# Diffusion step with a PEER expert mixer on one core: the V stage's third and fourth group are loaded ahead of the wait for all gate stores

## What is computed

```python
experts = (i1 * PEER_KEYS + i2).reshape(nch, PEER_CHUNK, PEER_HEADS * PEER_TOPK)
...
        h = jax.nn.gelu(jnp.einsum('tkd,td->tk', u[ec], xc))
        return jnp.einsum('tk,tkd->td', gc * h, v[ec])
```

## Time and profile before

| | |
|---|---|
| Median of 3 runs | 3056.86 us (3056.62 to 3060.37) |
| The profiled execution's own time | 3059.12 us |
| Its span | 3057.6 us |
| TensorE busy | 2904.8 us, 95% of the span |
| VectorE busy | 1813.5 us, 59% |
| ScalarE busy | 1203.6 us, 39% |
| V stage of layer 1 (first to last start of an L699 matmul) | 986.8 to 1518.7 us |
| V stage of layer 2 | 2498.7 to 3031.0 us |
| Mean granted clock of TensorE | 0.978 |

### The profile page before, as it was taken

One profiled execution on the slowest core, in us unless ns is written; L12 is line 12 of the kernel. 1 busy time (PEld: TensorE's weight loads), 2 busy tenths in 40 slices (PEclk: granted clock), 3 DMA queues, 4 the chain that ended last, 5 costly groups with the idle time before them and its releaser, 6 DMA issues.

```text
span 3057.6 us, 48767 instructions
## 1 busy us (share of the span) xinstructions
PE 2904.8 (95%) x16962; PEld 2660.9 (87%) x16962; DVE 1813.5 (59%) x4002; ACT 1203.6 (39%) x2024; POOL 10.0 (0%) x21
## 2 busy tenths in 40 slices
PE   6898999999999999999988989999999999999997
PEld 5877999999999788888778789999999997888886
DVE  3344387776875555555534444878777745555555
ACT  3343334344344344444323434443443433434443
POOL 0000000000000000000000000000000000000000
PEclk8998999999999999999989999999999999999999
DMA  6262353764847766666454524547558387666661
GB/s 272 104 235 86 121 177 120 221 195 132 261 153 239 277 227 219 226 229 222 151 218 145 186 84 142 162 129 239 179 153 260 116 276 269 227 219 226 230 221 64
DMA packets 256736, 581.68 MB, mean 190 GB/s; under 512 B 13025, under 2 KB 209889, under 8 KB 211617
## 3 DMA queue, kind: packets, MB, share of 16 engines
q1 hardware_dynamic: 255360, 571.81, 54.8%
q0 software_dynamic: 1184, 7.34, 0.6%
HBM read 475.82 MB, written 103.28 MB: 189 GB/s over the span
## 4 chain that ended last, share of the span: by engine, by line
PE 90%; DMA 3%; DVE 2%; issue 2%; ACT 1%; SPq 1%; ACTq 0%; DVEq 0%
PE ps L660 33%; PE ps L699 33%; PE ps L550 11%; PE ps L681 6%; PE ps L567 1%; PE ps L515 1%; PE ps L493 1%; PE ps L625 1%; PE ps L642 1%; DMA act_scratch<-act_h 1%; DMA gate_scratch<-g_all 1%; PE ps L614 1%; DMA wring<-in_w_ada_dram 1%; PE ps L595 1%; DVE u_lo L1150 0%
## 5 line engine op out<-in xcount | busy, mean ns | idle before, releaser
L660 PE MATMUL ps<-h_lo,u_hi 128*128 128x384 f32 x2048 | 697.0, 340 | 13.7 <-DVE u_lo L1150 5.8
L660 PE MATMUL ps<-h_hi,u_lo 128*128 128x384 f32 x2048 | 688.1, 336 | 0.0
L660 PE MATMUL ps<-h_hi,u_hi 128*128 128x384 f32 x2048 | 687.4, 336 | 0.0
L699 PE MATMUL ps<-v_lo,w_hi 128*128 128x512 f32 x1536 | 600.5, 391 | 15.8 <-DVE v_lo L1291 15.2
L1291 DVE TENSOR_TENSOR v_lo<-wring,v_hi 128x512 fp32r<-128x512 f32 x512 | 354.6, 693 | 435.6 <-ACT v_hi L924 435.4
L699 PE MATMUL ps<-v_hi,w_hi 128*128 128x512 f32 x1536 | 599.7, 390 | 0.0
L699 PE MATMUL ps<-v_hi,w_lo 128*128 128x512 f32 x1536 | 599.5, 390 | 0.0
L924 ACT CAST v_hi<-wring 128x512 fp32r<-128x512 f32 x512 | 316.8, 620 | 598.0 <-PE ps L699 597.9
L1150 DVE TENSOR_TENSOR u_lo<-wring,u_hi 128x1024 fp32r<-128x1024 f32 x256 | 313.2, 1223 | 208.7 <-ACT u_hi L881 205.3
L660 PEld LDWEIGHTS ps<-h_lo,u_hi 128*128 128x128 f32 x2048 | 386.5, 189 | 18.7 <-DVE u_lo L1150 10.3
L660 PEld LDWEIGHTS ps<-h_hi,u_hi 128*128 128x128 f32 x2048 | 386.5, 189 | 0.0
(11 more groups left out here) (162 smaller groups left out, 2971.8 us busy)
## 6 DMA issues: line engine op xcount, KB each, us to landing
wring<-in_u_t_dram SPq DMA_DIRECT2D x128, 1024.0 KB, 5.6
wring<-in_v_t_dram SPq DMA_DIRECT2D x128, 1024.0 KB, 4.9
wring<-in_w_ada_dram SPq DMA_DIRECT2D x48, 1024.0 KB, 6.8
act_scratch<-act_h SPq DMA_DIRECT2D x256, 192.0 KB, 5.8
gate_scratch<-g_all SPq DMA_DIRECT2D x48, 1024.0 KB, 6.4
gate<-gate_scratch SPq DMA_DIRECT2D x64, 768.0 KB, 6.3
act<-act_scratch SPq DMA_DIRECT2D x64, 768.0 KB, 7.9
wring<-in_w_in_dram SPq DMA_DIRECT2D x20, 1024.0 KB, 5.2
```

The lines of the kernel that those rows point to most:

```text
L660: last = nc.tensor.matmul(ps[:, 6 + s % 2, 0:T], u[:, s % 2, k], hx[:, k], start=(k == 0 and n == 0), stop=(k == KC - 1 and n == 2))
L699: last = nc.tensor.matmul(ps[:, bank + tb], w[:, group * G + b, cols], v[:, n % 4], start=(first and n in (0, G) and k == 0), stop=(last_u ...
```

## The change

Three edits, all in SyncE's list. Pieces 5, 6 and 7 are taken out of `TAIL_PIECES`. The definition of `group_loads` moves up, and it is called for groups 2 and 3 ahead of the wait for all stores; piece 5 is stored after group 2's loads, pieces 6 and 7 after group 3's. The loop over the other groups begins at 4. Because groups 2 and 3 are now loaded before the wait for all activation stores, the earlier wait on `act_st`, ahead of group 0's load, asks for the first 16 blocks where it asked for 8.

```diff
-TAIL_PIECES = {2: (3,), 3: (4,), 4: (5, 6, 7)}
+TAIL_PIECES = {2: (3,), 3: (4,)}
...
                     for sig in act_st:
-                        sp.wait_ge(sig.sem, sig.at(l, 16 * (2 * G // AR)))
+                        sp.wait_ge(sig.sem, sig.at(l, 16 * (4 * G // AR)))
                         sp.sem_inc(sp_passed.sem, 1)
...
+            def group_loads(g, n, ga=True):
+
+                if ga:
+                    sp.wait_ge(w32_rdy.sem, l * NB + (g - 1) * G)
+                    load_ga(g, n)
+                for half in range(2):
+                    slot = 2 * n + half
+
+                    sp.wait_ge(vlo_rdy.sem, l * NV + (g * (2 * G) + (G * (half - 3) + vlo_rdy.credit)))
+                    load_v(g, half, slot)
+
+            for n in range(2):
+                group_loads(2 + n, n)
+                for piece in ((5,), (6, 7))[n]:
+                    store_gates(TB - 1, piece)
             for sig in g_st[3:]:
                 sp.wait_ge(sig.sem, sig.at(l, 16 * TB))
                 sp.sem_inc(sp_passed.sem, 1)
...
-            with sp.Fori(1, NG // 2) as i:
+            with sp.Fori(2, NG // 2) as i:
                 for n in range(2):
                     group_loads(i * 2 + n, n)
```

More of the change, by code:

```diff
@@ L435, in _ @@
                     load_ga(1, 1)
[L436 to L441, removed]
             def group_loads(g, n, ga=True):
@@ L452, in group_loads @@
                     load_v(g, half, slot)
-            with sp.Fori(1, NG // 2) as i:
+            for n in range(2):
+                group_loads(2 + n, n)
+                for piece in ((5,), (6, 7))[n]:
+                    store_gates(TB - 1, piece)
+            for sig in g_st[3:]:
+                sp.wait_ge(sig.sem, sig.at(l, 16 * TB))
+                sp.sem_inc(sp_passed.sem, 1)
+            for sig in act_st:
+                sp.wait_ge(sig.sem, sig.at(l, 16 * (NB // AR)))
+                sp.sem_inc(sp_passed.sem, 1)
+            with sp.Fori(2, NG // 2) as i:
                 for n in range(2):
```

## The result

The changed kernel takes 3035.98 us (median of 6 runs, 3033.14 to 3040.92), the kernel before, run beside it, 3058.23 us (3055.54 to 3062.28). The ratio is 0.9929, with a 95% interval of 0.9916 to 0.9942: faster by 0.7%. Predicted were 3037.0 us and a range of 3033 to 3043. The profiled execution took 3040.92 us, the longest of the six.

The account below looks back on a forecast made before the run. TensorE, busy for 95% of the span, was taken to bound the kernel. Removing V-stage stalls of 9.7 + 10.1 = 19.8 us and adding 0 takes the profiled 3059.12 to 3039.3, or 3037.0 for the median; range 3033 to 3043.

Parts of the forecast that it names:

- What bounds, and what the stall costs: V stage: TensorE bounds; its stall at the eleventh unit costs 9.7 and 10.1 us in the two layers, 19.8 together.
- Group 2 in time: V stage: group 2's loads, issued ahead of pieces 5 to 7, land at about 1001, 5 us before due.
- The rival in which later transfers get ahead of it: V stage, group 2: later loads and piece 5 share the engines, landing 3.4 us late; 3048 us; chance 0.06.
- Group 4, the next in line: V stage: group 4, still behind the wait for all stores, is released at 1032.9 to 1033.5, due 1038.7.
- pieces 6 and 7 are written at 1024.1: V stage: stores at 345 GB/s and loads at 381, with the queue never dry, finish these two stores at 1024.1.
- the 5 us of spare: V stage: margin between group 4's forecast release, 1032.9 to 1033.5, and its due time, 1038.7.
- a sign of being right: V stage: the DMA stays at 345 GB/s or more until 1024.
- second rival: V stage, group 4: mixed writes and loads move slower, so group 4 lands late; 3053 us at 270 GB/s; chance 0.05.
- the allowance: SyncE before group 2's landing: with a full queue, an issue of the same load takes 2.34 us.
- A sign of being wrong that came up: V stage: VectorE waiting for `act<-act_scratch` 16 units further on, at about 1033, would show the second or third rival.
- third rival: V stage, group 4: SyncE goes on after 1039.6, costing more than the old stall; 3071 us at 222 GB/s; chance 0.03.
- The wait that moves to group 4: V stage: the wait for all stores makes group 4 late and costs what was won; 3053 us at 270 GB/s; chance 0.05.

Follow-up runs that it names:

- the changed kernel again: The changed kernel measured once more, nothing altered, as yardstick beside the later follow-up kernels: 3036.13 us, ratio 0.9936 to the kernel before.
- three more pieces: Against the changed kernel, pieces 5 to 7 stored a second time, into an unused tensor, behind piece 7 and ahead of group 4: 3049.51 us, ratio 0.9971.
- six more: Against the changed kernel, pieces 5 to 7 stored two extra times, into an unused tensor, ahead of group 4: 3070.41 us, ratio 1.0045.
- The first experiment: Against the kernel before, only the wait for all stores moved behind groups 2 and 3; pieces 5 to 7 still issued first: 3049.22 us, ratio 0.9971.

## Why the prediction was right

*What bounds, and what the stall costs.* Right to a tenth on the V stage: 19.8 us predicted, 9.7 + 10.1 measured. It was read from one execution by adding up matmul starts, idle time and slow matmuls together; the idle time alone (15.2 us in the earlier trace rows) would have been 4.6 us short. The medians of whole executions can't confirm it that closely: they differ by 22.3 us here and by 20.6 in the changed kernel again, so the total's being only 1.0 us off is in part luck.

*Group 2 in time.* Landing was worked out at about 1001 and VectorE was released at 1001.76. The trace shows at most 1.08 us of wait for group 2, and the changed kernel again 1.88, both well inside the slack of 5.45. The rival in which later transfers get ahead of it falls with this: three more transfers, 3.15 MB, stood right behind it. The profile before had shown that already, and that was the right row to trust, though its figure was somewhat small: the 0.24 MB were counted from 1008.8 on, and from the issue at 1006.97 to 1013.55 the queue moved 293 GB/s, 1.93 MB, which leaves up to 0.36 MB for transfers that got ahead.

*Group 4, the next in line.* Here one step was wrong in size: "pieces 6 and 7 are written at 1024.1". SyncE issued them at 1013.84, as forecast (about 1014), but they were written at about 1026.5. SyncE went on at 1029.64 and not at 1026.3 to 1026.9, and group 4 was released at 1036.19, not at 1032.9 to 1033.5. Of the 5 us of spare 3 were used, without effect on the time. Some 2.4 us come from the bytes: from 1015 to 1026 the queue moved 277 GB/s, where the prediction had set at least 345 until 1024 as a sign of being right, and had noted against its second rival that no stretch with a full queue shows less. The trace of before has short ones that do, which the earlier trace rows don't show: 299 GB/s from 968 to 970 and 279 from 2479 to 2481, both where loads were issued right behind stores and an issue of SyncE took 2.1 to 2.2 us. Some 0.6 us come from the time between the last byte and SyncE's going on, 3.1 us instead of 2.2 to 2.8. The 8.79 us for which the issue behind piece 5 was held were not foreseen either (2.34 us an issue was the allowance), but they ended before the slot was free that SyncE had to wait for, and cost nothing.

Why the stretch is slow isn't settled. The issues of the two pieces are held through most of it (8.93 us), but a held issue does not by itself lower the rate: with all three pieces behind group 3 they are held for 9.20 us while 329 GB/s are moved, and in the profile before for 7.19 us at 345. The rate also differs between executions of the same kernel: 307 GB/s in the changed kernel again (1013 to 1023).

*A sign of being wrong that came up.* The prediction named "a wait of VectorE for `act<-act_scratch` 16 units further on, at about 1033" as a sign that its second or third rival was true. VectorE does wait there, from 1033.81 to 1036.19, and neither rival came about. Of the second, its mechanism is there in part (the mixture of stores and loads moved slower from 1015 to 1026), but SyncE went on at 1029.64, ahead of the 1032.1 at which that rival begins to cost: TensorE doesn't wait and its clock stays at 1.00. The sign was drawn at the wrong engine. Up to 5.45 us of VectorE's wait are free, so the sign should have been a wait of TensorE, or one of VectorE of more than that.

*The other rivals.* The wait that moves to group 4 is real as a mechanism: three more pieces bring it about and cost 13.5 us (3049.51 less 3035.98), six more make the kernel slower than before. As the kernel stands, the wait at group 4 could grow by some 3 us before TensorE stood: the slack of 5.45 us less the 2.38 of VectorE's wait. The first experiment shows that both parts of the old stall counted: keeping the bytes ahead of group 2 and dropping only the wait wins 7.8 us of the 20.6 (medians, each against the kernel before beside it: 3056.99 less 3049.22, and 3056.7 less 3036.13 for the changed kernel).

## What to carry to other kernels

When a queue has to pass a wait for many stores, ask for each load behind it whether it needs that wait. Give the loads that are due first their own place ahead, and the stores the time in which the queue has room. Then work out what is due next: the wait is still there, and what counts is how many us of spare it has before the next load that needs it. Leave room in that spare, since the queue moved 277 GB/s for 11 us in the new order where 345 or more had been counted on; look for short dips in the old trace too. A stall of TensorE can cost more than its idle time: those of 3.8 to 13.4 us here cost 1.7 to 3.1 us more, because it comes back slow. But in this kernel a load may be 5 us late for VectorE before TensorE stands at all, so read the spare at the engine that bounds the kernel.

## What the runs showed of the hardware

The slow clock after a stall didn't grow with the stall's length: 3.1 us after 3.8 us idle, 1.7 after 4.30, 2.5 after 4.60, 2.4 after 7.29 and 1.7 after 13.24 (the stage's time over 522.2 less the idle time, the 3.8 being layer 2 of the kernel with three more pieces). The other three stalls, of 4.75, 7.92 and 13.41 us, fit in with 1.8, 2.2 and 1.7. After 0.43 us the next matmul took 0.49 us, and none ran at half the clock. An issue on SyncE behind a gate store (1024 KB) and two loads can be held long: 8.79 us for one that takes 0.39 us without that store ahead. While it is held SyncE issues nothing else, as its list runs in order. It cost nothing here, as SyncE's next point, the slot at about 1013.8, came later; where a load is due sooner, a store's place in the order may cost the issuing queue too, which no run here shows.
